# One slice of lag instead of two before the last product of the narrow experts

## The reference

```
def swiglu(x, w_gate, w_up, w_down):
    return (jax.nn.silu(x @ w_gate) * (x @ w_up)) @ w_down
```

## Time and profile before

| | us |
|---|---|
| median of three runs | 1436.52 |
| profiled execution, its own time | 1437.85 |
| span of the profiled execution | 1436.0 |
| PE busy | 1384.0 (96%) |
| DVE busy | 893.0 (62%) |
| ACT busy | 697.5 (49%) |

### The profile page before, as it was taken

The page is one execution under the profiler, slowest core; times in us unless marked ns, Lnnn a source line. Parts: engine busy times, 40 slices in busy tenths (PEclk is TensorE's granted clock), DMA queues, the critical chain, the costliest instruction groups (busy, mean ns, idle before and its releaser), DMA issues.

```text
span 1436.0 us, 19041 instructions
## 1 busy us (share of the span) xinstructions
PE 1384.0 (96%) x7514; PEld 1059.8 (74%) x7514; DVE 893.0 (62%) x1026; ACT 697.5 (49%) x771; POOL 58.3 (4%) x99
## 2 busy tenths in 40 slices
PE   9999999999999999999989999899999999999996
PEld 8898888888888889888867766566665665666675
DVE  6788977555545778897687545444444453445487
ACT  6347644544445336663576434433345343345374
POOL 2000000000000000000210000000000000000002
PEclk9999999999999999999999999999999999999999
DMA  8545554455454644554779999999999999999994
GB/s 339 208 149 182 191 184 176 148 212 198 179 200 172 214 164 166 188 183 165 279 293 353 402 420 422 409 422 420 422 408 421 421 421 421 420 421 421 421 420 159
DMA packets 79423, 424.20 MB, mean 295 GB/s; under 512 B 9248, under 2 KB 9424, under 8 KB 45536
## 3 DMA queue, kind: packets, MB, share of 16 engines
q1 hardware_dynamic: 72864, 402.16, 70.6%
q0 software_dynamic: 6048, 20.15, 4.2%
q10 hardware_dynamic: 416, 0.60, 0.1%
HBM read 414.48 MB, written 8.39 MB: 294 GB/s over the span
## 4 chain that ended last, share of the span: by engine, by line
PE 72%; DMA 18%; DVE 4%; ACT 3%; issue 2%; SPq 0%; POOL 0%; DVEq 0%; POOLq 0%
PE ps L909 22%; DMA late<-experts_dram 14%; PE ps L1462 9%; PE ps L1208 8%; PE ps L1414 5%; PE ps L886 5%; PE ps L1472 5%; PE ps L897 5%; DMA raw_m<-experts_dram 4%; PE ps L1185 4%; DVE w_lo L2153 2%; PE ps L1425 1%; ACT w_hi L1654 1%; ACT w_hi_x L1654 1%; DVE w_lo_x L2153 1%
## 5 line engine op out<-in xcount | busy, mean ns | idle before, releaser
L2013 DVE TENSOR_TENSOR w_lo<-raw_m,w_hi 128x2048 fp32r<-128x2048 f32 x113 | 257.7, 2288 | 111.3 <-ACT w_hi L1580 111.3
L1580 ACT CAST w_hi<-raw_m 128x2048 fp32r<-128x2048 f32 x113 | 214.6, 1906 | 126.3 <-PE ps L909 56.2
L2153 DVE TENSOR_TENSOR w_lo<-late,w_hi 128x2048 fp32r<-128x2048 f32 x59 | 135.0, 2289 | 97.2 <-ACT w_hi L1654 97.0
L909 PE MATMUL ps<-w_hi,hT_hi 128*128 128x512 f32 x464 | 183.1, 395 | 0.0
L909 PE MATMUL ps<-w_hi,hT_lo 128*128 128x512 f32 x464 | 180.9, 390 | 0.0
L909 PE MATMUL ps<-w_lo,hT_hi 128*128 128x512 f32 x464 | 180.7, 389 | 0.0
L1654 ACT CAST w_hi<-late 128x2048 fp32r<-128x2048 f32 x59 | 112.4, 1905 | 79.9 <-DMA late<-experts_dram 77.6
L1462 PE MATMUL ps<-w_hi,hT_hi 128*128 128x512 f32 x268 | 112.9, 421 | 19.2 <-DVE w_lo L2153 18.2
L2153 DVE TENSOR_TENSOR w_lo<-raw_m,w_hi 128x2048 fp32r<-128x2048 f32 x40 | 91.6, 2289 | 44.0 <-ACT w_hi L1654 44.0
L1414 PE MATMUL ps<-late,light_x 128*64 128x256 f32 x896 | 109.6, 385 | 0.0
L1462 PE MATMUL ps<-w_lo,hT_hi 128*128 128x512 f32 x268 | 107.3, 400 | 0.0
(11 more groups left out here) (428 smaller groups left out, 2538.0 us busy)
## 6 DMA issues: line engine op xcount, KB each, us to landing
late<-experts_dram SPq DMA_DIRECT2D x165, 1024.0 KB, 14.4
raw_m<-dense_dram SPq DMA_DIRECT2D x226, 512.0 KB, 4.1
raw_m<-experts_dram SPq DMA_DIRECT2D x99, 1024.0 KB, 14.0
bias<-b_in_dram POOLq DMA_DIRECT2D x26, 256.0 KB, 5.8
late<-dense_dram SPq DMA_DIRECT2D x4, 512.0 KB, 9.8
raw_m<-front_dram SPq DMA_DIRECT2D x4, 384.0 KB, 4.5
raw_m<-front_dram SPq DMA_DIRECT2D x2, 768.0 KB, 7.3
x_rows<-prow POOLq DMA_DIRECT2D x3, 512.0 KB, 10.9
```

The lines of the kernel that those rows point to most:

```text
L909: ins = mm(ps[:, b, :], hT[a][:, k, t * P:(t + 1) * P], wsp[r][:, s, kk * W:(kk + 1) * W], start=(k == 0 and pa == 0), stop=(k == KT - 1 a ...
L1580: copy(w_hi[:, g % RS, :], slot_raw(g, False)).then_inc(hi_ready, 1)
L2013: tt(w_lo[:, g % RS, :], slot_raw(g, False), w_hi[:, g % RS, :], ALU.subtract)\
L2153: tt(lo_slot(j), slot_raw(m, True), hi_slot(j), ALU.subtract).then_inc(lo_ready, 1)
```

## The change

Lines 139 and 149. The light stream is built with a lag of one slice, and one left-over light step instead of two is placed among the last heavy steps:

```diff
-    hs, ls = steps(HEAVY, 1), steps(LIGHT, 2)
+    hs, ls = steps(HEAVY, 1), steps(LIGHT, 1)
...
     for n in range(TAIL + 1):
         MS0 += hs[nh0 + n]
-        if n < 2:
+        if n < 1:
             MS0 += ls[len(LIGHT) * NF + n]
```

## The result

The changed kernel takes 1440.56 us in the median of 8 runs (1438.93 to 1441.97), the kernel before 1436.92 us, timed beside it (8 runs, 1436.23 to 1438.43): ratio 1.0024, 95% interval 1.0013 to 1.0035. Forecast were 1437.1 us and "the same"; the time lies above the range (1440.0). The profiled execution took 1441.61 us (before: 1437.85), span 1439.8 (1436.0), mean granted clock 0.986 (0.991).

What follows compares the result with a forecast made beforehand. Weight loads were taken to bound the kernel, PE only 3% faster in a full round. The middle of the clock's outcomes gave about +0.6 us on the span, 1437.1 us on the median; range 1435.4 to 1440.0.

Steps and rivals of the forecast that it cites:

- the same: Whole kernel: time not measurably different from before, within about 0.2%, 2.9 us; chance 0.82.
- A light product at the ten places: Ten places in the expert block: PE 2.83 us behind after each added wait, hidden by slack; cost 0, bounds 0 to 28 us.
- the queue rival: Light chunks left later empty the load queue: 1.46 us a hole, 4.4 at three places; 1442 us likeliest; chance 0.11.
- The last places: Tail: PE ends 0.87 us later, about 0.1 us seen at the end; bounds -0.5 and +1.4.
- the fourth gather: At the end: starts after the addition behind the last load, not after the light rows; DVE waits 1.50 us for it.
- The start of the stream: Loads at 811 to 819 us: a slot freed sooner makes every later landing 0.5 us earlier; upper bound 1.46 us.
- The clock: PE at 237: open whether the clock falls; 1.6 us seen at the end with a fall, otherwise 0.1.
- The sum: Whole kernel: about +0.6 us on the profiled span, 1436.0 to 1436.6; on the median 1437.1 us.
- clock at every place: Rival: the clock falls at all ten places, nine falls hidden, the last seen; 1438.1 to 1439 us; chance 0.14.

Runs made afterwards that it cites:

- the first run: Changed kernel, but at all ten places ACT copies the transposed light rows before casting the heavy chunk three positions on: 1440.10 us, ratio 1.0022.
- the sixth run: Changed order up to position 242, with the last two light products back at 249 and 253 as in the kernel before: 1439.77 us, ratio 1.0022.
- the eleventh: Changed order up to 242, tail from the kernel before, ACT's copy ahead of the cast only at the last place (light product at 237): 1437.02 us.
- old_order_new_tail: Order of the kernel before up to position 242, then the changed tail (last two light products at 243 and 250): 1440.18 us, ratio 1.0020.
- old_order_wait: Kernel before, plus a PE wait at the ten places for the cast of the heavy chunk two positions on: 1438.04 us, ratio 1.0008.
- run 14: Changed kernel with the first gather held until chunk 258 is split and ACT's copy first at the last place only: 1438.44 us, ratio 1.0009.
- run 9: Changed kernel with ACT's copy first at all ten places and the first gather held until chunk 258 is split: 1437.36 us, ratio 1.0000.
- run 4: Changed kernel, but the last light product stands at position 253, as before the change, instead of 250: 1439.84 us, ratio 1.0021.
- copy_first: Kernel of the first run: changed kernel with ACT's copy ahead of the cast at all ten places, 1440.10 us.
- copy_first_gathers_held: Kernel of run 9: changed kernel with ACT's copy first at all ten places and the first gather held until chunk 258 is split, 1437.36 us.
- new_order_old_tail: Kernel of the sixth run: changed order up to 242, then the tail from the kernel before, 1439.77 us.

## Why the prediction was wrong

**A light product at the ten places: the mechanism right, "cost while the queue holds: 0" wrong at two places.** Forecast was a start about 2.1 us after the landing two on; measured 2.11. PE's lag did not add up over the places, as said. The queue lost more than the 2.8 us: the shortest issue to landing fell from 9.1 to 7.3 us and the DMA engines went empty at the two hand-overs; by 1400 us 3.1 us of transfer are missing. That is the queue rival at two places instead of three, and at about the size it was given (1.5 us each), but by the first run it was not what set the end: with the queue whole, 1440.10.

**The last places: the step that failed.** It said that PE ends 0.87 us later and 0.1 us are seen, and that the last light rows are stored three positions earlier *too*, as a help. The last load was to land 0.3 to 0.9 us earlier. It landed 4.0 us later, and PE ended 4.0 us later. Given the landings, PE's arithmetic held: from the heavy chunk at 1354.39, 14.37 us to 1368.76 and 50.95 to 1419.71; measured 1368.76 and 1419.46. What failed is what was put in for the loads. They were not 0.5 us earlier but 1.6 late at the last place, for which the queue was priced at 0. And the earlier store released POOL's gathers 5.05 us earlier (1397.04), whose transfers go in ahead of the last weights. Of the 4.0 us by which the last load is late, 2.7 are there at position 253, and 1.2 arise behind it (29.17 against 27.93 us): in the kernel before, too, the gathers delay the last loads, only less. I named who waits for the store and forgot whom its follower pushes back: I priced the fourth gather, which comes behind the last load, and not the three ahead of it, though they were in the trace.

**PE's lag before the tail.** The step gave 1.4 us as the upper bound of what is seen, and put a fall of the clock at 1.6 us more. The sixth run against the eleventh puts 2.7 us on the last place (1439.77 to 1437.02). Right was the reason: behind it heavy steps stand together, and what PE is behind there stays, while nine waits ahead of it are nearly free.

**The start of the stream: 0.5 us that were not there.** The term was read from 406 GB/s at 811 to 819 us in the trace of before. After has 424 there, but the change can't be credited with it: `old_order_new_tail` and `old_order_wait`, which have the order of before at this place, ran at 426 and 421. None of the fifteen other traces is under 421 there: the 406 belong to that one execution. Nothing landed earlier: after was 0.13 MB behind at 820 us, and `old_order_new_tail` 0.15. After:

```profile
811.00:819.00 8.00, 8.00 (x52) 4.67 (x52) 6.74 (x5) 4.68 (x5) 0.00 (x0) 1.00 1.01 424
801.00:806.00 5.00, 5.00 (x23) 3.22 (x20) 4.13 (x3) 1.96 (x2) 0.00 (x0) 1.00 0.95 269
```

**The clock.** The sum took +0.6 us. From the prediction's own values, 0.1 us without a fall and 1.6 with one at four in nine, it would be 0.8; that slip changes nothing here. The wait before the tail was put at up to 3.7 us, where its own terms (1.77 + 2.83 - 0.5) give 4.1; it was 3.22. The matmuls ran slow at six of the ten places, and at the last one they did not (1.94 us for the product) in the trace of after; in the sixth run they did. Three places of the trace of after, PE over time:

```profile
852.94 3.46 PE L1425 MATMUL ps<-raw_m,light_y 128*64 128x512 f32 x8 [3.36 <-ACT light_y L1878]
...
999.30 1.94 PE L1425 MATMUL ps<-late,light_y 128*64 128x512 f32 x8 [1.08 <-ACT light_y L1878]
...
1208.66 1.94 PE L1425 MATMUL ps<-late,light_y 128*64 128x512 f32 x8 [2.41 <-ACT light_y L1878]
```

The granted clock is 0.50 at 853 to 856 us and 1.00 at the other two products and at the last (1352.6 to 1354.4). With a fall the product took 3.03 to 3.68 us, 1.1 to 1.7 more than 1.94 (forecast: 1.6), but the wait's length alone does not decide it: 3.22 us without a fall, 3.12 with one in the same trace (at 1261.53), 1.67 with one in the sixth run's. The Trainium skill, "TensorE: Matmul & The Clock Gate", section "HAM oscillation — how this bites in real kernels", says of a loop whose matmuls wait for a load at each turn that every turn starts on the lower clock. Read as a rule it would have all ten fall; the trace agrees at six and disagrees at four. Three of these four waits (1.08, 1.71 and 2.41 us) are shorter than the waits of about 3 to 5 us that the section tells of, so it bears on the fourth (3.22) only. The rival "clock at every place" was wrong in its condition, and its effect alone would not have made the time.

**What the sum missed.** Two chains were 0.80 us apart in the kernel before. The sum followed one and let the other run as given. Now both are 3.7 to 4.0 us late, and the end moved by 3.8 us in the span: their later one, not their sum.

**Not settled.** How much of what is left in run 14 (1.9 us, against 0.5 in run 9) is the queue's running down and how much the other nine waits; and why the kernels with PE as the later chain spread more from run to run (1437.64 to 1442.94 in the sixth) than those with the loads. A clock that falls at one of the late places in some runs and not in others would fit: in runs 4 and 6 the slower executions mostly have the lower mean clock (the five slow ones of run 4 0.982 to 0.986, the fastest 0.990). Where it fell in them isn't on record, so the place is a guess.

## What to carry to other kernels

Where work is moved earlier, follow everything that it releases, on every queue: a store moved up by three positions sent three gathers ahead of the last weights. Where an engine's program is in order, a small copy behind an instruction that waits for a load is itself a wait for that load, and its price depends on the place: little where slack follows, nearly all of it where the work behind is continuous. Where two chains end within a microsecond, price both, and test by taking both away: holding the gathers alone brought 1.3 us (1438.94), with the other chain repaired 2.9 (1440.10 to 1437.36), and half of the change cost nearly as much as the whole (1440.18, 1439.77). And a term read from one stretch of one trace has to be looked for in a second: the 406 GB/s were there once.

## What the runs showed of the hardware

- Indirect gathers issued by POOL delay weight loads that SP issued about as early: 1.57 MB of them moved into the last ten loads' stretch made it 29.2 us (`copy_first`) instead of 25.7 (`copy_first_gathers_held`). The Trainium skill, "DMA: Bandwidth & Descriptors", section "Issuing engines are not separate DMA queues", says that DMAs of different issuers run on the same 16 engines and interleave; the traces agree, with the full time of the gathers' bytes.
- A median of 12.6 us from issue to landing, five beats, did not keep the engines fed in the trace of after: the share went to 0.91 and 0.92 at 1068 and 1276 us, where loads issued at that time landed after 7.7 and 7.4 us (about 3 beats). A short time from issue to landing is no sign by itself: the shortest of all, 7.3 us, was issued at 1170 us, and 1170 to 1174 us ran at a share of 1.01 and 416 GB/s.
- A wait of 3.22 us in front of the product at the last place left the clock at 1.00 in one trace (after); one of 1.67 us in front of the same product had it at 0.50 in another (`new_order_old_tail`, 1353.4 to 1356.6 us).
